# Removing TensorE's filler products at the stage seams and in the routing of a two-block model kernel

## The reference, cut to what matters

```python
for l in range(DEPTH):                       # DEPTH = 2
    x = x + hybrid_mixer(rms_norm(x, norm_mix[l]), ...)
    h = rms_norm(x, norm_ffn[l])
    if l % 2 == 0:
        x = x + swiglu(h, ffn_wg[i], ffn_wu[i], ffn_wd[i])
    else:                                     # logits -> top 2 -> gates -> experts
        x = x + moe_swiglu(h, moe_router[i], moe_wg[i], moe_wu[i], moe_wd[i])
x = rms_norm(x, norm_final)
```

## Time and profile before

| what | value |
|---|---|
| median of three timed runs | 1464.2 us |
| the profiled execution's own time | 1462.07 us |
| its span, first to last instruction | 1460.2 us |
| around the span (1462.07 less 1460.2) | 1.9 us |
| TensorE busy | 1422.4 us, 97% |
| mean granted TensorE clock | 0.995 |

### The profile page before, as it was taken

One profiled execution on the slowest core, in us unless ns is written; L12 is line 12 of the kernel. 1 busy time (PEld: TensorE's weight loads), 2 busy tenths in 40 slices (PEclk: granted clock), 3 DMA queues, 4 the chain that ended last, 5 costly groups with the idle time before them and its releaser, 6 DMA issues.

```text
span 1460.2 us, 19942 instructions
## 1 busy us (share of the span) xinstructions
PE 1422.4 (97%) x7982; PEld 1223.7 (84%) x7982; DVE 1106.4 (76%) x938; ACT 906.0 (62%) x775; POOL 90.2 (6%) x130
## 2 busy tenths in 40 slices
PE   6999999999998999999999999999999999999998
PEld 6879999897787888888888888888878869688896
DVE  6966454389688889788888888888878894657665
ACT  5564444356656677777777777767767765655653
POOL 3400000034001000000000000000002110000000
PEclk9999999999999999999999999999999999999999
DMA  9569985355559999999999999999999965333341
GB/s 321 181 209 284 318 281 188 117 179 173 173 212 368 372 384 384 359 405 350 377 391 337 414 378 354 397 355 387 371 357 374 393 212 173 103 129 116 117 173 58
DMA packets 120979, 409.63 MB, mean 281 GB/s; under 512 B 7027, under 2 KB 32867, under 8 KB 120913
## 3 DMA queue, kind: packets, MB, share of 16 engines
q1 hardware_dynamic: 114432, 392.32, 73.6%
q0 software_dynamic: 5408, 12.58, 2.7%
q10 hardware_dynamic: 1072, 3.80, 0.7%
HBM read 399.53 MB, written 18.87 MB: 287 GB/s over the span
## 4 chain that ended last, share of the span: by engine, by line
PE 84%; DVE 10%; DMA 2%; ACT 2%; issue 1%; POOL 0%; SPq 0%; ACTq 0%; DVEq 0%; POOLq 0%
PE ps L496 22%; PE ps L498 22%; PE ps L497 22%; DVE yT L2038 3%; DVE low L480 3%; PE ps L1180 2%; PE ps L1182 2%; PE ps L1181 2%; PE ps L2739 1%; PE ps L1390 1%; PE ps L1388 1%; PE ps L1389 1%; DMA sgu_o<-in_sgu_nb 1%; PE ps L1360 1%; DMA raw<-in_w_in 1%
## 5 line engine op out<-in xcount | busy, mean ns | idle before, releaser
L486 DVE TENSOR_TENSOR low<-raw,high 128x2816 fp32r<-128x2816 f32 (+1 forms) x168 | 516.3, 3089 | 98.6 <-ACT high L475 98.5
L475 ACT ACTIVATE high<-raw 128x2816 fp32r<-128x2816 f32 (+1 forms) x168 | 428.9, 2562 | 110.4 <-PE ps L498 57.1
L496 PE MATMUL ps<-high,xT_hi 128*128 128x512 f32 (+1 forms) x1136 | 419.9, 370 | 8.4 <-DVE low L480 4.1
L498 PE MATMUL ps<-high,xT_lo 128*128 128x512 f32 (+1 forms) x1136 | 416.2, 366 | 0.0
L497 PE MATMUL ps<-low,xT_hi 128*128 128x512 f32 (+1 forms) x1136 | 414.7, 365 | 0.0
L480 DVE TENSOR_TENSOR low<-raw,high 128x2816 fp32r<-128x2816 f32 (+2 forms) x72 | 202.5, 2819 | 76.2 <-ACT high L469 74.6
L496 PEld LDWEIGHTS ps<-high,xT_hi 128*128 128x128 f32 x1136 | 213.7, 188 | 41.5 <-DVE low L480 5.9
L469 ACT ACTIVATE high<-raw 128x2816 fp32r<-128x2816 f32 (+3 forms) x71 | 166.8, 2351 | 118.6 <-PE ps L498 91.6
L497 PEld LDWEIGHTS ps<-low,xT_hi 128*128 128x128 f32 x1136 | 213.9, 188 | 28.2
L498 PEld LDWEIGHTS ps<-high,xT_lo 128*128 128x128 f32 x1136 | 213.5, 188 | 28.0
L496 PE MATMUL ps<-high,eT_hi 128*128 128x512 f32 x352 | 140.7, 400 | 0.0
(11 more groups left out here) (437 smaller groups left out, 1864.0 us busy)
## 6 DMA issues: line engine op xcount, KB each, us to landing
raw<-in_moe_wg SPq DMA_DIRECT2D x64, 1408.0 KB, 8.3
raw<-in_moe_wu SPq DMA_DIRECT2D x64, 1408.0 KB, 9.3
raw<-in_moe_wd SPq DMA_DIRECT2D x48, 1536.0 KB, 8.5
rawb<-in_w_in SPq DMA_DIRECT2D x25, 1024.0 KB, 5.1
raw<-in_w_in SPq DMA_DIRECT2D x16, 1024.0 KB, 9.3
raw<-in_moe_wd SPq DMA_DIRECT2D x16, 1024.0 KB, 8.5
raw<-in_ffn_wg SPq DMA_DIRECT2D x8, 1408.0 KB, 10.4
raw<-in_ffn_wu SPq DMA_DIRECT2D x8, 1408.0 KB, 13.1
```

The lines of the kernel that those rows point to most:

```text
L475: nc.scalar.activation(high[:, j % SPLITS, 0:n], raw[:, j % RAWS, 0:n], ACT.Copy).then_inc(hi_made, 1)
L486: nc.vector.tensor_tensor(low[:, j % SPLITS, 0:n], raw[:, j % RAWS, 0:n], f(high[:, j % SPLITS, 0:n]), ALU.subtract).then_inc(lo_made, 1)
L496: nc.tensor.matmul(out, xh, wh, start=first, stop=False)
L498: return nc.tensor.matmul(out, xl, wh, start=False, stop=last)
```

## The change

Both helpers and all their calls are removed. Nothing is added or moved, and the waits between the calls stay as they were.

```diff
-    def keep_warm(bank, count):
-
-        for _ in range(count):
-            nc.tensor.transpose(ps[:, bank, 0:P], ident, ident)
...
                 for b in range(NB):
                     norm_transposes(2 * l, 2 * l, b)
-                    if l and b == 0:
-                        keep_warm(3, 24)
...
                 if j == 0:
-                    keep_warm(3, 10)
                     norm_transposes(1, 1, 0)
...
-            def wide_filler(count):
-
-                for _ in range(count):
-                    nc.tensor.matmul(ps[:, 3, :], xT_hi[:, 0, 0:P], high[:, MOE0 % SPLITS, 0:512], start=True, stop=True)
-
-            keep_warm(3, 10)
             norm_transposes(3, 3, 0)
             pe.wait_ge(x_made, 12)
             pe.wait_ge(hi_made, MOE0 + 1)
             pe.wait_ge(xt_hi, 12 + 1)
-            wide_filler(3)
             router_product(0)
-            wide_filler(4)
             norm_transposes(3, 3, 1)
-            wide_filler(5)
             router_product(1).then_inc(logits_ready, 1)
-            wide_filler(11)
             pe.wait_ge(chosen_made, 1)
...
-            wide_filler(7)
             pe.wait_ge(xs_lo, 2)
```

## The result

Thirteen timed runs of each kernel, side by side: 1464.43 us before and 1473.53 us after (medians); the ratio is 1.0053, 95% interval 1.0039 to 1.0067, so about 7.8 us more. (The ratio is estimated from all the runs; the two medians divided give 1.0062, which lies inside the interval.) The forecast was 1465.2 in a range of 1461.6 to 1469.5. The time lies outside the range, on the slower side, which had 30%.

A forecast was written before the change was run, and what follows sets the result against it. TensorE was taken as the bound, busy 97% of the span with 84% of the chain. Routing -0.1, second seam +1.1 and first seam 0 gave +1.0 us on 1464.2: 1465.2, range 1461.6 to 1469.5.

The forecast's parts named there:

- The sum for the full clock: Routing without fillers at an unchanged clock: logits 2.2 us earlier, about 0.3 more before the gather, together -2.5 us.
- VectorE's order limits the logits: Routing, block 1: VectorE's own sequence of work sets the logits copy at about 400.15 against 402.39, 2.2 us earlier.
- The fall of the clock: Routing: with nothing wide running before the gather, 1.2 GHz from 396 at the latest into the gather.
- Half of it at the low clock costs +1.1: The routing's gather, 3.54 us at 2.4 GHz: half slow costs +1.1 us, bounds 0 and +3.5 (a doubling).
- The factor 1.6: Assumed slowdown at 1.2 GHz for router products, place products (+0.8 us) and the gather (5.7 us if wholly slow).
- The routing's ledger: Routing: -2.5 + 0.5 (turnings and router) + 0.8 (place products) + 1.1 (gather) = -0.1 us, bounds -2.5 and +2.8.
- Expert 0: First chunk: 1 us of low clock there would cost 0.5 us, of which `low` on VectorE hides some 0.3.
- Second seam: Without its 24 fillers TensorE idles 3.1 us and the clock may fall under products on the chain: +1.1 us.
- First seam: Idle times of 1.15 and 0.54 us, less than an earlier stop that kept the clock: 0, upper bound +1.7 us.
- The second: Rival, 27%: every seam's dense products start at half speed; first +1.7, second +1.7, routing +0.8, total +4.2, 1468.4 us.
- The first: Rival, 12%: the clock holds or costs nothing, so the full 2.5 us gain comes, 1461.7 us.
- The third: Rival, 5%: expert 0's late-chunk transfer swallows the routing's difference, leaving the second seam's +1.1, 1465.3 us.

The follow-up runs named there:

- the fitted kernel: Kernel before with three added filler groups, and the routing's 30 wide products cut to 24 placed in waits; ratio 0.9990 against the kernel before.
- the three variants with a slow gather: Against the kernel before: all routing fillers out, 1.0049; only its last two groups (11 and 7) out, 1.0061; those 18 narrowed to 8 columns, 1.0032.
- two variants: Kernel before without the routing's first groups (10, 3, 4, 5), 1.0017; kernel after with only the 11 and 7 wide products put back, 1.0041 against before.
- the routing-only variant: Kernel before with only the routing's fillers removed (10 transposes, 3+4+5+11+7 wide products); ratio 1.0049.
- The single removals: Kernel before without the first seam's ten transposes, 1.0003; without the second seam's 24, 1.0036 and 1.0018; without the routing's fillers, 1.0049.

## Why the prediction was wrong, step by step

**The sum for the full clock came out near.** I had -2.5 us for the routing with the fillers off the chain; the fitted kernel, whose clock held, has -2.43, with its logits copied 2.3 us earlier where I had 2.2. It still issues 24 fillers, so it tests the sum only in part. The prediction's words "at an unchanged clock" do not fit either: the sum takes every product at full speed and so also counts as gain the 3.4 us low stretch of the earlier trace rows; that alone is worth 1.6 of it (19.70 against 18.12), and the fillers themselves, at the full clock, the other 0.9. That the seams' fillers were hidden holds: without them TensorE waits 1.15 and 3.08 us for `xn`. That VectorE's order limits the logits is not shown: in the fitted kernel VectorE and TensorE are done with the work ahead of the copy within 0.04 us of each other, and in the kernel after it is TensorE's slow products that end last.

**The fall of the clock was right, its length was not.** The prediction said "Half of it at the low clock costs +1.1" for the gather. All of it was at the low clock, at twice the time: +3.5, the upper bound that I had written down. I had assumed that the clock rises somewhere within the gather. In the kernel after and in the three variants with a slow gather, it rose only behind it, 2 to 5 us into expert 0's products: the low stretch lasted 20.5 us in the kernel after, where I had let it end halfway through the gather. With 11 wide products at half speed ahead of it, in two variants, it was back before. So the step that failed is the point at which the clock rises, not the fall.

**The factor 1.6 was too low.** It came from eight transposes at 188 ns each, from 398.03 to 399.53, but the clock was back from 399.2, so the last of them were not slow. The same eight transposes took 1.97 in the kernel after, eight router products 1.71 against 0.79, ten place products 2.3 (406.59 to 408.90) against 1.26, the gather 7.06 against 3.54: a factor near 2, 214 ns for each product of 128, 16 or 8 columns. The loads themselves slowed down, as the gather's rows show, before and after (duration in ns minimum/median/maximum):

```profile
L2673 PEld LDWEIGHTS ps<-pick,xn_lo x16: 192/192/192, 408.0 to 411.0; 128*128 128x128 f32 x16
L2654 PEld LDWEIGHTS ps<-pick,xn_lo x16: 333/333/333, 411.0 to 416.8; 128*128 128x128 f32 x16
```

The Trainium skill, "TensorE: Matmul & The Clock Gate", section "LDWEIGHTS (loading the stationary operand)", gives the load of P columns as P / 1.2 ns, 107 ns for 128, and names no clock beside it; the prediction took that as the same at either clock. By that reading, an estimate from the page's figure, the gather would have stayed near 3.5. The 214 ns from product to product, and the loads at 333 in place of 192, speak against it here.

**The routing's ledger** (from the turning of block 0): logits copied at 9.68 us in place of 10.89, so 1.2 earlier where I had 1.7; places +1.05 where I had +0.8; the gather's start 0.3 nearer behind `pick`, as forecast; the gather +3.5 where I had +1.1. Together about +3.0 (2.93 by the cuts) in place of -0.1, and the gather is 2.4 of the 3.1 between them.

**Expert 0.** I had 0.5 less 0.3 for a low clock reaching into its first chunk, and then put nothing in the sum for it. It reached 2.0 us in, and the way to the late chunk grew by 1.5. ScalarE's `high` became the wait, as the chain shows: `high` of the fourth chunk runs from 422.19 and the third `low` behind the gather waits for it; before, it ran from 415.34 and was hidden behind the first two. In the routing-only variant it was +2.0.

**Second seam**: +1.1 forecast; +1.2, +1.05, +1.08 and +1.2 measured in profiles. Right in size there; the timed runs say somewhat more.

**First seam**: 0 forecast with +1.7 as bound. +1.3 in two of three profiles, nothing measurable on average when it is removed alone. The comparison with the stop of the earlier trace rows, by which a shorter idle time should leave the clock alone, did not hold: 1.15 and 0.54 us of idle time stood ahead of the fall here.

**The sum.** By the profiles: routing +2.9 for -0.1, expert 0 +1.5 for nothing, first seam +1.3 for 0, second +1.2 for +1.1: 6.9 us in place of 1.0.

**The rivals.** The second, in which each seam starts its stage at 1.2 GHz, is what happened in the profile, with low stretches from 108.5 and 303.1, both under products; they cost 1.3 and 1.2 rather than its 1.7 each. It priced the routing at +0.8 where 4.4 (2.9 and 1.5) came. The first, a clock that holds or costs nothing, is refuted for the bare kernel. The third, that the experts absorb the difference, is refuted too: the way to the late chunk grew. My range ended just past a rival whose own routing term was mis-sized by 3.6 us. The bounds in my own text, +2.8 for the routing, +1.7 and +1.7 for the seams, added up to 1470.4; I had cut them off.

**What stays open.** The single removals (0.03%, 0.18 to 0.36%, 0.49%) sum to 0.7 to 0.9%, the full removal gives 0.53% (0.39 to 0.67). Runs of one kernel spread over some 9 us (1460.79 to 1470.15 before), so these can't be told apart surely. Nor was it tried why the late chunk's stop differs between 1.3 and 4.4 us. Each variant was profiled once or twice, and low stretches come and go between executions, so single differences of 1 to 2 us in a profile can be such a stretch. And no run separates the width of the fillers from the unbroken work that they give TensorE.

## What to carry to other kernels

Price a filler by the slowest work behind it at either clock, not by whether it lies on the chain: 18 wide products, mostly in waiting time, saved a gather of 3.5 us from doubling. When a low clock is foreseen, do not end it at the next product of any kind: in these traces it lasted through narrow ones and ended under wide ones. Fill mostly the waiting time: with 24 wide products in place of 30, fitted to the waits, the routing was 0.85 us shorter in the profile than with all 30 at the same full clock. In the timed runs that gain is not to be seen, and the clock was low for longer than with all 30 (14 against 10 us on average).

Before crediting an edit with a difference of 1 to 2 us in one profile, look for a low stretch that one of the two happened to have.

## What the runs showed of the hardware

- Products of 8, 16 and 128 columns doubled in time at the low clock, though their columns are few: 0.214 us each against 0.10 to 0.11.
- Eighteen products of 8 columns in the place of 18 of 512 left the clock to fall (in the one profile taken; they also left 1.25 us of idle time); a gather of 32 products of 128 columns at 1.2 GHz ran to its end without a rise, in four profiles (7.06 us three times, and 6.93). Behind the second seam the clock rose under products of 256 columns (kernel after: 0.88 in 306 to 308).
- A weight load of 128 columns took 192 ns at 2.4 GHz and 333 ns at 1.2 GHz in the gather.
- Whether a given short wait lowers the clock differs between executions of near-equal kernels: in the ten profiles in which the second block is untouched, its 2.00 us wait had a low stretch behind it seven times; in the six in which the routing is untouched, its low stretch came five times.
